# Two transformer blocks on one core: the end of the second mixture with its last weights in halves, columns in halves, and sums on the residual rows

## The reference

```python
def hier_moe(h, w_group, b_group, w_expert, b_expert, w_gate, w_up, w_down):
    ...
    combine = jnp.sum(jax.nn.one_hot(global_i, N_EXPERTS_2, dtype=F32) * top_w[..., None], axis=1)
    out = jnp.zeros(hf.shape, F32)
    for e in range(N_EXPERTS_2):
        hid = jax.nn.silu(t @ w_gate[e]) * (t @ w_up[e])
        out = out + combine[:, e:e + 1] * (hid @ w_down[e]).astype(F32)
    return out.reshape(bsz, seq, d).astype(h.dtype)

def hybrid_layer(...):
    ...
    x = x + merged @ w_out
    x = x + hier_moe(rms_norm_2(x, g_ffn), w_group, b_group, w_expert, b_expert, w_gate, w_up, w_down)
    return x
```

## Time and profile before

| | |
|---|---|
| time, median of 3 runs | 2243.97 us (2236.05 to 2248.34) |
| profiled execution | 2246.94 us |
| its span | 2245.1 us |
| mean granted clock of TensorE | 0.919 |
| PE busy | 1842.2 us, 82% |
| DVE busy | 812.1 us, 36% |
| ACT busy | 497.7 us, 22% |
| HBM read, written | 709.35 MB, 1.07 MB |
| DMA queue of SP (q1) | 77.1% of 16 engines' span |

### The profile page before, as it was taken

How to read it: one execution, slowest core, us unless ns; L and a number is a source line. 1 busy time by engine, 2 the same in 40 slices (tenths; PEclk the granted TensorE clock), 3 DMA queues, 4 the chain that set the end, 5 groups by cost and what they waited for, 6 DMA issues and landing times. The chain is left out here.

```text
span 2245.1 us, 28438 instructions
## 1 busy us (share of the span) xinstructions
PE 1842.2 (82%) x11560; PEld 837.4 (37%) x11560; DVE 812.1 (36%) x1624; ACT 497.7 (22%) x1008; POOL 77.1 (3%) x96
## 2 busy tenths in 40 slices
PE   7899999899999989789987897698888845666555
PEld 3655545433433333234333232254534512222221
DVE  2224333333442344334443333587682300000001
ACT  2022311223232133332333333321301200000000
POOL 0000000000000000000000000093000000000000
PEclk9999999899999999889999999799999878787777
DMA  7744349498898799999999999443128299999996
GB/s 273 279 152 167 131 161 351 159 425 355 328 421 365 283 424 423 423 423 396 423 422 424 422 424 422 148 145 120 41 94 339 98 429 427 427 428 427 427 428 259
DMA packets 113958, 713.56 MB, mean 318 GB/s; under 512 B 16703, under 2 KB 21007, under 8 KB 68655
## 3 DMA queue, kind: packets, MB, share of 16 engines
q1 hardware_dynamic: 105344, 704.98, 77.1%
q10 hardware_dynamic: 8398, 5.47, 0.8%
HBM read 709.35 MB, written 1.07 MB: 316 GB/s over the span
## 5 line engine op out<-in xcount | busy, mean ns | idle before, releaser
L841 PE MATMUL ps<-ring,ar 128*32 128x512 f32 x3072 | 377.1, 631 | 62.4 <-DMA ring<-in_w 42.9
L459 PE MATMUL ps<-ar 128*128 128x128 f32 (+5 forms) x1742 | 352.9, 359 | 29.1 <-PEq L737 5.7
L466 PE MATMUL ps<-ring,ar 128*32 128x512 f32 x1184 | 208.7, 713 | 157.9 <-DMA ring<-in_w_gate 79.6
L459 PEld LDWEIGHTS ps<-ar 128*128 128x128 f32 (+2 forms) x1742 | 233.4, 200 | 154.0 <-issue 105.2
L459 PE MATMUL ps<-ring,ar 128*128 128x512 f32 (+2 forms) x592 | 248.4, 579 | 5.1 <-ACT ar L2201 2.6
L841 PEld LDWEIGHTS ps<-ring,ar 128*32 128x32 f32 x3072 | 97.2, 113 | 334.9 <-issue 264.1
L1738 DVE TENSOR_SCALAR ar<-ps 128x256 f32<-128x256 f32 x128 | 54.3, 425 | 438.3 <-PE ps L841 429.0
L853 PE MATMUL ps<-ring,ar 128*32 128x512 f32 x1536 | 175.1, 602 | 0.0
L574 PE MATMUL ps<-ring,ar 128*128 128x512 f32 x384 | 171.7, 597 | 0.0
L459 PEld LDWEIGHTS ps<-ring,ar 128*128 128x128 f32 x592 | 112.8, 192 | 134.3 <-issue 127.7
L2322 ACT ACTIVATE ar<-ps 64x512 f32<-64x512 f32 x256 | 151.5, 592 | 46.6 <-PE ps L853 32.5
(11 more groups left out here) (396 smaller groups left out, 1377.5 us busy)
## 6 DMA issues: line engine op xcount, KB each, us to landing
ring<-in_w SPq DMA_DIRECT2D x192, 2048.0 KB, 20.9
ring<-in_w_gate SPq DMA_DIRECT2D x26, 2048.0 KB, 26.0
ring<-in_w_up SPq DMA_DIRECT2D x24, 2048.0 KB, 26.2
ring<-in_w_down SPq DMA_DIRECT2D x24, 2048.0 KB, 24.0
ring<-in_w_in SPq DMA_DIRECT2D x21, 2048.0 KB, 8.1
ring<-in_w_ada SPq DMA_DIRECT2D x12, 2048.0 KB, 8.1
ar<-in_w_up SPq DMA_DIRECT2D x8, 2048.0 KB, 25.7
ar<-in_w_down SPq DMA_DIRECT2D x8, 2048.0 KB, 28.8
```

The lines of the kernel that those rows point to most:

```text
L459: ins = self.t.e.matmul(o, l, r, start=(i == 0), stop=(i == len(pairs) - 1))
L466: ins = self.t.e.matmul(b[32 * i:32 * i + 32, :], l, r, start=(k == 0), stop=(k == len(steps) - 1))
L841: ins = e.matmul(b[32 * s:32 * s + 32, :], HG[:, 2 * c + r, 32 * n:32 * n + 32], W[:, r, HALF(s)], start=False, stop=(c == 3 and r == 1))
```

## The change

- The last four weights, w_down of unit 7, come as eight DMAs: row groups 0 and 1 of each first, then row groups 2 and 3 of each. The second ones count on a semaphore of their own, `s_rest`.
- TensorE's `l2_2` of the last unit goes by row groups: groups 0 and 1 for both halves of the columns, then a wait for `s_rest`, then groups 2 and 3.
- The spread of the last unit goes by halves of the columns, both row blocks of h = 0 first, and waits for the eviction of its half alone.
- In the second mixture VectorE adds onto XV, where the residual rows are, instead of YV. YV isn't cleared, and the two additions at the end are gone; the leftover path adds onto XV too.
- SP stores four blocks of 128x512, in the order in which they are summed, each when its last sum is done.

```diff
+        def rest(name, src, *shape):
+
+            q.e.dma_start(RG_(held.index(tag + name), SLOT // 2, *shape), src).then_inc(s_rest, 16)
+        return fetch, rest
...
-            fetch((nm, u, i), a[nm][0, 4 * u + i].rearrange("(p r) n -> p r n", r=r), r, SLOT // r,
-                  lane=(lanes[k % 9],))
+            src = a[nm][0, 4 * u + i].rearrange("(p r) n -> p r n", r=r)
+            if k < len(units) - 4:
+                fetch((nm, u, i), src, r, SLOT // r, lane=(lanes[k % 9],))
+            else:
+
+                fetch((nm, u, i), src[:, 0:2, :], 2, 1024, lane=(lanes[k % 9],))
+                last.append(((nm, u, i), src[:, 2:4, :]))
+        for name, src in last:
+            rest(name, src, 2, 1024)
         sync_past2(q)
 
-        for tb in range(2):
-            q.wait_ge(s_dve, dve["out", tb])
-            q.e.dma_start(out[0, 128 * tb:128 * tb + 128, :], XV[:, tb, :]).then_inc(s_out, 16)
-        q.wait_ge(s_out, 32)
+        for h, tb in ((0, 0), (0, 1), (1, 0), (1, 1)):
+            q.wait_ge(s_dve, dve["sum", 2, NE // 4 - 1, 0, tb, h])
+            q.e.dma_start(out[0, 128 * tb:128 * tb + 128, HALF(h)], XV[:, tb, HALF(h)]).then_inc(s_out, 16)
+        q.wait_ge(s_out, 64)
...
+            if u == NE // 4 - 1:
+                tensor_last(t, w, W, AT_, rows)
+                break
...
-        spread(t, w, 2, NE // 4 - 1, TL2)
+
+    def tensor_last(t, w, W, AT_, rows):
+
+        u = NE // 4 - 1
+        bs = [w.claim("l2_2", u, h, lane=YL) for h in range(2)]
+        for g in range(2):
+            if g == 1:
+                t.wait_ge(s_rest, 64)
+            for h in range(2):
+                for r in (2 * g, 2 * g + 1):
+                    for i in range(4):
+                        ins = t.e.matmul(bs[h][32 * i:32 * i + 32, :], AT_[:, r, rows[i]], W[i][:, r, HALF(h)],
+                                         start=(r == 0), stop=(r == 3))
+                if g == 1:
+                    pe["l2_2", u, h] = t(ins)
+        for h in range(2):
+            t.wait_ge(s_act, act["yg", 2, u, h])
+            for tb in range(2):
+                b = w.claim("sp", 2, u, 0, tb, h, lane=TL2)
+                pe["sp", 2, u, 0, tb, h] = w.sums(b[:, :], [(SWT2[u % 2][:, 0, TB(tb)], YG2[:, HALF(h)])])
...
-        for tb in range(2):
-            dve["out", tb] = v(v.own.tensor_tensor(XV[:, tb, :], XV[:, tb, :], YV[:, tb, :], ALU.add))
...
-            o = YV[:, tb, HALF(h)]
-            v(v.own.tensor_tensor(o, ps("sp", m, u, i, tb, h)[:, :], o, ALU.add))
+            o = (YV, XV)[m - 1][:, tb, HALF(h)]
+            dve["sum", m, u, i, tb, h] = v(v.own.tensor_tensor(o, ps("sp", m, u, i, tb, h)[:, :], o, ALU.add))
...
-        v(v.own.memset(YV, 0.0))
...
-            act["yg", 2, u, 0] = n
+                if u == NE // 4 - 1:
+                    act["yg", 2, u, h] = n
+            if u < NE // 4 - 1:
+                act["yg", 2, u, 0] = n
```

More of the change, by code:

```diff
@@ L120, in build @@
                  for i in range(2)]
-    s_pb, s_bb = sem("s_pb"), sem("s_bb")
+    s_pb, s_bb, s_rest = sem("s_pb"), sem("s_bb"), sem("s_rest")
     s_px, s_py, s_ps = sem("s_px"), sem("s_py"), sem("s_ps")
@@ L315, in fetch @@
             slot[tag + name], wts[tag + name] = i, count[i]
-        return fetch
+        def rest(name, src, *shape):
+            q.e.dma_start(RG_(held.index(tag + name), SLOT // 2, *shape), src).then_inc(s_rest, 16)
+        return fetch, rest
     def sync(q):
-        fetch = fetcher(q, s_w, s_pe)
+        fetch, rest = fetcher(q, s_w, s_pe)
         d1 = (0, 1, 2, 3)
@@ L411, in sync @@
         lanes = (3, 4, 5, 6, 8, 7, 2, 0, 1)
+        last = []
         q.wait_ge(s_pe, pe["sy", 3])
@@ L1157, in sync_past1 @@
             r.e.dma_start(B1P, a["b1"][0]).then_inc(s_pb, 16)
-            fetch = fetcher(r, p_w, p_pe, ("past1",))
+            fetch, _ = fetcher(r, p_w, p_pe, ("past1",))
             for x in range(NE):
@@ L1167, in sync_past2 @@
         with Region(q, 2, None) as r:
-            fetch = fetcher(r, p_w, p_pe, ("past2",))
+            fetch, _ = fetcher(r, p_w, p_pe, ("past2",))
             for x in range(NE):
@@ L1662, in add @@
         def add(i, tb, h):
-            o = YV[:, tb, HALF(h)]
-            v(v.own.tensor_tensor(o, ps("sp", m, u, i, tb, h)[:, :], o, ALU.add))
+            o = (YV, XV)[m - 1][:, tb, HALF(h)]
+            dve["sum", m, u, i, tb, h] = v(v.own.tensor_tensor(o, ps("sp", m, u, i, tb, h)[:, :], o, ALU.add))
             read["sp", m, u, i, tb, h] = v.mark()
[L1667 to L1670, removed]
+        order = [(tb, h) for tb in range(2) for h in range(2)]
+        if m == 2 and u == NE // 4 - 1:
+            order = [(tb, h) for h in range(2) for tb in range(2)]
+        for tb, h in order:
+            v.wait_ge(s_pe, pe["sp", m, u, 0, tb, h])
+            add(0, tb, h)
         def second_half():
```

## The result

The changed kernel took 2234.0 us (median of 5 runs, 2230.46 to 2235.14) against 2243.97 us of the kernel before (five runs by then, 2236.05 to 2248.34, the same median as of the first three). The ratio is 0.9954, with a 95% interval of 0.9934 to 0.9974: faster, by 10.0 us, and by a little less than the 0.5% that had been drawn as the line; the interval reaches from 5.8 to 14.8 us. The forecast was 2232.9 us.

A forecast was written before the change was run, and what follows sets the result against it. The weight stream bounds the second mixture, so only the 22.1 us behind the last landing can shrink, to 11.0: matmuls 3.5, spread 3.74, add 0.70, store 2.45, small terms. Gain 11.1 us gives 2232.9 us, range 2226 to 2241.

The forecast's parts named there:

- the 0.5% that had been drawn as the line: Smallest difference a measurement tells from no change, about 11.2 us or 2232.75 us; faster by over 0.5% given 0.45.
- First halves land in order and early: Last w_down tiles: first halves land at about 2213.2 us, so 32 of 64 matmul instructions run under the stream.
- The first rival: Weight stream's end: engines mix the eight transfers, all land near 2223; 5.0 us less gained, 2237.9 us; chance 0.04.
- 8 KB pieces: Last four weight tiles: halving 16 KB pieces delays the last landing by 0 to 0.8 us; 0.35 us taken.
- toll per transfer: Rival, full weight queue: each of four added transfers costs extra, 2238.5 us or up to 2240.9; chance 0.03.
- The clock: TensorE behind the last landing: full clock after a 1.7 us pause, 32 instructions in 3.5 us; a dip costs 1.4 more.
- The eviction: Ahead of the last unit's spread: TensorE's 0.67 us wait for the second half's eviction goes with the order by columns.
- Branch and additions: VectorE's end: the 2.65 us branch over the leftover path and 2.48 us of 128x1024 adds leave the path.
- The stores: Kernel's end: a 256 KB store takes 2.05 us to landing and 2.45 to the end, where before it was 3.15.
- the branch's bound: VectorE's branch behind its last sum, beside the store: nothing added for it, at most 0.3 us.
- the stores queue up: Rival, kernel's end: four stores of 2 KB pieces in a row end 1.8 us later, 2234.7 us; chance 0.05.

The follow-up runs named there:

- the sums: Kernel before with only the second mixture's sums put onto the residual rows, two 512 KB stores kept; ratio 0.9984, 18.0 us from last landing to end.
- the halves: Kernel before with only the last four weights in halves and l2_2 by row groups; ratio 0.9969, 17.0 us from last landing to end.
- the version by columns: Changed kernel with the last four weights in four parts, the first half of the columns finished ahead of the last landing; 2232.61 us, ratio 0.9952.

## Why the prediction was right, and where it was not

The forecast gain was 11.1 us; the profiles have 10.3 us of it and the medians 10.0. That the median fell within 1.1 us of the forecast is in part luck, as its interval is some 9 us wide; the mechanism is borne out by the profiles. From SP's issue on the stores cost 1.1 us more than summed, and 0.3 us came back in other terms, 0.2 of them because the last landing was 0.15 us later in this pair of traces and not 0.35. The steps, one by one:

- *First halves land in order and early.* Right. The 32 early instructions have no wait for a DMA, and the pause behind them is 1.5 us (1.7 forecast). The first rival fell.
- *8 KB pieces.* 0.35 us allowed. In the six traces with halves the last landing is 29.9 to 30.1 us behind SP's issue, in the three with whole weights 29.6 to 29.7: 0.3 us on average. No toll per transfer: less than 0.1 us for each of the four more.
- *The clock.* Right: 1.00 behind a pause of 1.5 us, 0.58 behind one of 5.9 us, at a price of 1.2 us. The 32 take 3.6 us (3.5 forecast).
- *The eviction.* 0.67 us forecast; TensorE waits 0.72 us for it where the order by columns is undone, and not at all in the change.
- *Branch and additions.* 5.13 us off the path, as forecast; the kernel before without the path shows that the 2.65 us were the branch.
- *The stores.* This is the term that was mis-sized: "2.05 to landing, and 2.45 to the end". Measured are 2.9 us in the median and 3.6 us to the end. The price of 2.05 was right for what it priced, four stores of 256 KB by themselves (2.1 us without the path). The failed step is the branch "beside the store's 2.45": I had compared its length with the stores', 2.65 with 2.45 us, and added nothing. What I did not see is what it does to them while it runs beside them. The branch jumps over a long piece of code, and loads of instructions go with it through the 16 DMA engines, each 16 KB about 1.1 us of one engine's time (two loads, 2.0% of 16 engines in 6.7 us); in the kernel before they were over when the stores began. This costs 1.1 us, more than the 0.3 us that the prediction set as the branch's bound, and took back a tenth of the gain. The rival that priced "the stores queue up" at +1.8 us (1.95 by its own terms, 4 x 1.3 - 2.6 - 0.65) had the place right and the reason wrong.

By the Trainium skill, *DMA: Bandwidth & Descriptors* ("Why a DMA increments its semaphore by 16 and not by 1"), the engines of a transfer finish independently and the semaphore is full when the last has reported, so one held-up engine is enough. The runs agree, 2.1 against 2.9 us for the same store without and with such loads, and the tail at 24 GB/s. The fixed cost of about 2.0 us per DMA in the same page of the Trainium skill ("Anatomy of one DMA", where it is given for DMAs that GpSimd issues) makes an estimate of 2.6 us for a store of 256 KB. Measured are 2.1 us without the loads, so the prediction's 2.05 from rows was the better price. In the full queue no such cost shows: four transfers more, in smaller pieces, cost 0.3 us in all.

By size, then, the change stands just inside 0.5% by its median; the interval of 0.26 to 0.66% lies on both sides of that line. The two parts tried alone gave 4.1 us (the sums) and 5.1 us (the halves) in the profiles, and the order by columns 0.9, single traces each: together 10.2 of the 10.5 us that the change has behind the last landing. The three runs leave out the four stores in place of two, which the run with two stores prices at 0.6 to 0.8 us by one trace; the parts can't be added up more closely than that.

## What to carry to other kernels

Where a kernel ends with a stream of weights, look first at what follows the last landing: split the last transfers so that most of the work on them is done when the last one lands, and keep the matrix engine's pause short. Splitting further pays only until the engine's own work since its last operand became ready is the longer path; reckon that sum before the parts are made smaller. Work taken off the path does not vanish: ask what it does to the DMA engines at its new place, code loads behind a branch included.

## What the runs showed of the hardware that was not expected

- Loads of instructions behind a branch over long code share the DMA engines with the stores: the same 512 KB store lands 2.7 us after its issue without them in its time, and 3.6 to 4.0 us with them; a 256 KB store 2.1 us without and 2.9 to 3.1 us with them where the four follow each other by 0.86 us (medians of each trace).
- An issue on SP can take microseconds by itself. The eighth half weight's took about 3.0 us (the last pair 3.49 us, other pairs 0.91), and in the version by columns one pair took 10.85 us. By the landings two whole weights and seven halves were on their way when the 3.0 us began. That may be a limit on transfers under way, which is not shown: no run was made for it. It cost nothing here, as the stream stayed full.
